# Fourier stage and first scores of the first tower's attention, put in another order

## The reference

```
y_f = fourier_mix(zf, w_fourier)      # Re(2-D DFT over positions and group channels), then @ w_f
q   = rms_norm(cq) @ w_uq             # 8 heads, 64 + 32 rope channels
k,v = rms_norm(ckv) @ w_ukv           # k gets the shared rope part kr
p   = softmax((qn.kn + rope(qr).kr) * scale);  attn = p @ v
y_c = conformer_conv(zg)              # 31-tap depthwise conv, LayerNorm, silu, pointwise
x   = x + gate * (concat([y_f, attn, y_c]) @ w_o)
```

## Time and profile before

| what | value |
|---|---|
| median of 3 runs | 2862.61 us (2860.85 to 2864.79) |
| the profiled execution | 2860.66 us, its span 2858.9 us |
| PE busy | 2749.6 us (96%) |
| DVE, ACT, POOL busy | 1693.3, 1108.4, 1123.5 us (59%, 39%, 39%) |

### The profile page before, as it was taken

One profiled execution on the slowest core, in us unless ns is written; L12 is line 12 of the kernel. 1 busy time (PEld: TensorE's weight loads), 2 busy tenths in 40 slices (PEclk: granted clock), 3 DMA queues, 4 the chain that ended last, 5 costly groups with the idle time before them and its releaser, 6 DMA issues.

```text
span 2858.9 us, 39941 instructions
## 1 busy us (share of the span) xinstructions
PE 2749.6 (96%) x14626; PEld 2217.2 (78%) x14626; DVE 1693.3 (59%) x2428; ACT 1108.4 (39%) x1815; POOL 1123.5 (39%) x533
## 2 busy tenths in 40 slices
PE   6999899999999999999999999899999999999998
PEld 3855688888888756788887688668888888888887
DVE  4978676564646577486678654856634643533133
ACT  4346533121222436542223523664433444443242
POOL 1399323333332277144444321003444434344443
PEclk8999999999999999999999999999999999999999
DMA  7600043333333320034454221003544532233332
GB/s 286 208 6 1 1 148 118 109 127 114 122 118 119 110 96 1 31 133 162 162 191 148 95 67 38 1 10 102 203 150 147 183 113 88 83 94 96 96 96 81
DMA packets 83492, 303.81 MB, mean 106 GB/s; under 512 B 9120, under 2 KB 12704, under 8 KB 82464
## 3 DMA queue, kind: packets, MB, share of 16 engines
q1 hardware_dynamic: 83072, 298.43, 30.8%
q10 hardware_dynamic: 288, 3.55, 0.3%
HBM read 299.84 MB, written 2.10 MB: 106 GB/s over the span
## 4 chain that ended last, share of the span: by engine, by line
PE 55%; DVE 6%; ACT 2%; issue 2%; POOL 0%; DVEq 0%; ACTq 0%; POOLq 0%
PE psum L1954 15%; PE psum L1751 10%; PE psum L1352 9%; PE psum L1975 8%; PE psum L1391 2%; PE psum L1829 1%; PE psum L1442 1%; PE psum L1610 1%; DVE psum L2112 1%; DVE in_lo L2105 1%; PE psum L1850 1%; DVE tiny L2620 1%; PE psum L1671 1%; DVE hidden_lo L2482 1%; PE psum L1657 1%
## 5 line engine op out<-in xcount | busy, mean ns | idle before, releaser
L642 POOL TENSOR_TENSOR w_lo<-w_raw,w_hi 128x1024 fp32r<-128x1024 f32 x346 | 868.3, 2510 | 1700.4 <-ACT w_hi L708 1700.2
L708 ACT ACTIVATE w_hi<-w_raw 128x1024 fp32r<-128x1024 f32 x346 | 366.9, 1060 | 1226.3 <-PE psum L1751 542.3
L2217 DVE CUSTOM_DVE_ANT_0 mod_w<-mod_w,conditions 128x1024 f32<-128x1024 f32 x176 | 287.4, 1642 | 4.4
L2198 DVE SCALAR_TENSOR_TENSOR residual<-psum,modulation,residual 128x512 f32<-128x512 f32 (+1 forms) x152 | 101.1, 684 | 316.6 <-PE psum L1975 143.3
L1954 PE MATMUL psum<-in_hi,w_hi 128*128 128x512 f32 x672 | 262.6, 391 | 4.4 <-DVE small_w L2704 2.5
L1954 PE MATMUL psum<-in_lo,w_hi 128*128 128x512 f32 x672 | 262.3, 390 | 0.0
L1954 PE MATMUL psum<-in_hi,w_lo 128*128 128x512 f32 x672 | 262.1, 390 | 0.0
L1751 PE MATMUL psum<-hidden_hi,w_hi 128*128 128x256 f32 (+1 forms) x736 | 223.1, 356 | 2.6 <-DVE hidden_lo L2482 2.2
L1751 PE MATMUL psum<-hidden_lo,w_hi 128*128 128x256 f32 (+1 forms) x736 | 222.2, 355 | 0.0
L1751 PE MATMUL psum<-hidden_hi,w_lo 128*128 128x256 f32 (+1 forms) x736 | 222.2, 355 | 0.0
L1751 PE MATMUL psum<-in_hi,w_hi 128*128 128x256 f32 (+1 forms) x720 | 215.5, 354 | 2.2 <-POOL w_lo L642 2.2
(11 more groups left out here) (330 smaller groups left out, 5778.1 us busy)
## 6 DMA issues: line engine op xcount, KB each, us to landing
w_raw<-stream_dram SPq DMA_DIRECT2D x346, 512.0 KB, 4.2
mod_w<-mods_dram SPq DMA_DIRECT2D x176, 512.0 KB, 3.7
mixer_space<-first_mods_dram SPq DMA_DIRECT2D x12, 512.0 KB, 14.5
small_w<-small_w_dram SPq DMA_DIRECT2D x2, 2048.0 KB, 13.1
in_hi_space<-dft_x_dram SPq DMA_DIRECT2D x2, 2048.0 KB, 8.8
residual<-tokens_dram ACTq DMA_DIRECT2D x1, 3072.0 KB, 10.6
in_lo_space<-first_mods_dram SPq DMA_DIRECT2D x4, 512.0 KB, 16.0
conditions<-conditions_dram SPq DMA_DIRECT2D x2, 1024.0 KB, 11.4
```

The costliest lines, as they stand in the source:

```text
L642: nc.gpsimd.tensor_tensor(wlo[:, (j % 2) * 1024:(j % 2 + 1) * 1024], raw3[:, j, :], whi[:, (j % 2) * 1024:(j % 2 + 1) * 1024].bitcast(F32) ...
L708: nc.scalar.activation(whi[:, (j % 2) * 1024:(j % 2 + 1) * 1024], raw3[:, j, :], ACT.Copy).then_inc(hi_ready, 1)
L2198: last = nc.vector.scalar_tensor_tensor(res3[:, m, s0:s1], bank(2 * (t % 2) + b, c1=s1 - s0), M(block_, chunk, m, 1 - b), res3[:, m, s0:s1 ...
L2217: nc.vector.tensor_tensor_reduce(w_tile, w_tile, cvec[:, 0:D], 1.0, 0.0, ALU.mult, ALU.add, dots[:, q:q + 1]).then_inc(mod_done, 1)
```

## The change

Four things move, on three engines; nothing is added to the work or taken from it, and the queues of POOL and SP are the same.

PE: the projections of the Fourier stage stand behind each position part `y`, no longer ahead of it. `scores(1)` moves from behind the products with `w_f` to ahead of them, `scores(2)` from the loop (d = 1) to behind the products, ahead of `turn(0)`. ACT: `proj_ev` moves with its projections, `exps(1)` moves from the loop (d = 0) to between the copies of the two products. DVE: `minimum(1)` moves from the loop to a place of its own in `TAPS_BEFORE` (`second`): in layer 0 three taps behind `weigh(0)`, with three more taps behind it; in layer 1 behind `rope1`. All of this holds for both layers, as the code is shared.

```diff
--- before.py
+++ after.py
@@ -444,8 +444,8 @@
             return sum(w(x) for _, x in group[:i])
 
         LN_FROM = (19, 12)
-        TAPS_BEFORE = [dict(queries=0, rope0=11, rope1=12, minimum=14, weigh=15, fourier=21),
-                       dict(queries=15, rope0=30, minimum=TAPS, weigh=TAPS, rope1=TAPS, fourier=TAPS)]
+        TAPS_BEFORE = [dict(queries=0, rope0=11, rope1=12, minimum=14, weigh=15, second=18, fourier=21),
+                       dict(queries=15, rope0=30, minimum=TAPS, weigh=TAPS, rope1=TAPS, second=TAPS, fourier=TAPS)]
 
         def fourier_out(m, seg):
 
@@ -979,20 +979,23 @@
                 segs = both(cols)
                 pieces = early_pieces(layer, 2 * len(segs))
                 for c in range(2):
-                    for _ in segs:
-                        for n in pieces.pop(0):
-                            proj_ev(n)
+                    for n in pieces.pop(0) if len(segs) > 1 else ():
+                        proj_ev(n)
                     if c:
                         exps(0)
                     act.wait_ge(s["y_mm"], c + 1)
                     for seg, _ in segs:
                         last = nc.scalar.activation(yf[:, c, seg[0]:seg[1]], fourier_out(c, seg), ACT.Copy)
                     last.then_inc(s["y_cp"], 1)
+                    for n in pieces.pop(0):
+                        proj_ev(n)
                 for m in range(2):
                     act.wait_ge(s["f_mm"], m + 1)
                     for seg, _ in segs:
                         last = nc.scalar.activation(hi3[:, m, seg[0]:seg[1]], fourier_out(m, seg), ACT.Copy)
                     last.then_inc(s["f_hi"], 1)
+                    if m == 0:
+                        exps(1)
                 for d in range(n_units + 1):
                     if d:
                         ev(d - 1)
@@ -1002,7 +1005,7 @@
                         proj_ev(before[d])
                     if d == n_units:
                         conv_silu()
-                    if d + 1 < n_units:
+                    if d and d + 1 < n_units:
                         exps(d + 1)
                     if d:
                         pv_hi(d - 1)
@@ -1618,8 +1621,6 @@
                 pieces = early_pieces(layer, 2 * len(segs))
                 for c in range(2):
                     for seg, _ in segs:
-                        for n in pieces.pop(0):
-                            project(n)
                         if c == 0:
                             pe.wait_ge(late["dft"], 32 * (layer + 1))
                         first, table = (0, dft_c) if seg == CTX else (2, dft_x)
@@ -1631,9 +1632,11 @@
                                                   256 * c + 128 * part + 128],
                                                table[:, part, k, :], start=(k == 0 and part == 0),
                                                stop=(k == nk - 1 and part == 1))
-                    mm.then_inc(s["y_mm"], 1)
-                    if c == 0:
-                        scores(0)
+                        if seg == segs[-1][0]:
+                            mm.then_inc(s["y_mm"], 1)
+                        for n in pieces.pop(0):
+                            project(n)
+                    scores(c)
                 for m in range(2):
                     for c in range(2):
                         if m == 0:
@@ -1642,7 +1645,7 @@
                             mm = pe.matmul(fourier_out(m, seg), wf[:, m, c, :],
                                            yf[:, c, seg[0]:seg[1]], start=(c == 0), stop=(c == 1))
                     mm.then_inc(s["f_mm"], 1)
-                scores(1)
+                scores(2)
                 pe.wait_ge(s["f_lo"], 2)
 
                 def turn(u):
@@ -1694,7 +1697,7 @@
                         mm.then_inc(s["ln"], 1)
 
                 for d in range(n_units + 1):
-                    if d and d + 1 < n_units:
+                    if d > 1 and d + 1 < n_units:
                         scores(d + 1)
                     if d in before:
                         project(before[d])
@@ -2411,7 +2414,7 @@
                         last.then_inc(s["ln"], 1)
 
                 steps = dict(rope0=lambda: rope_q(0), rope1=lambda: rope_q(1),
-                             minimum=lambda: minimum(0), weigh=lambda: weigh(0))
+                             minimum=lambda: minimum(0), weigh=lambda: weigh(0), second=lambda: minimum(1))
                 for step, until in TAPS_BEFORE[layer].items():
                     if step in steps:
                         taps(until)
```

## The result

The changed kernel takes 2875.35 us (median of 5 runs, 2873.43 to 2887.93) against 2861.49 us of 5 runs of the kernel before beside it: ratio 1.0052 (95%: 1.0037 to 1.0067), slower by 0.4 to 0.7%.

What follows compares the result with a forecast made beforehand. PE, busy 96% of the span, was taken as the bound, so only its waits and low clock count. Layer 1's +11.3 and layer 0's -1.7 us gave +9.6, forecast 2872.3 us, range 2866 to 2879.

Steps and rivals of the forecast that it cites:

- layer 1's bare chain: Layer 1: uncovered rotation before unit 0's scores +5.0, exponentials before unit 2's +2.6, copy before the loop's keys projection +1.4 us.
- its -1.7: Layer 0's net term: 3.0 us gained at the first value product, only 1.7 kept; bounds -7.0 and +1.3.
- the step: Layer 1, unit 0's scores: copy and rotation of head 0's queries no longer covered by the position part, +5.0 us.
- The copy of piece 3: Layer 1, ahead of head 0's query projection: PE waits for ACT to copy out the keys projection's bank, 0.6 us.
- The first clock fall: Layer 1, behind the 4.8 us idle time at unit 0's scores: the clock falls, +2.95 us, bounds 0 and 3.2.
- rival 1: More clock falls, at layer 1's unit 2 scores or layer 0's waits: +3.0 us (2875.3) or +6 (2878.3), called 2877; chance 0.27.
- the forecast's case: Whole kernel: layer 1 +11.3 us with one clock fall, layer 0 -1.7, in all 2872.3 us; chance 0.50.
- the cap: Layer 0's first LayerNorm sum: it waits for POOL's last tap, which doesn't move, so PE can gain only 1.7 us.
- Waits predicted 1.3, 1.7 and 0.8 us: Layer 0: PE waits ahead of unit 2's scores, at the turn for `lo3`, and at the first value product for ACT's copy.
- The upper bound of layer 0: Layer 0: waits around the short turn lower the clock, 3.7 us of work runs at half speed; +1.3 us.
- Rival 3: Not slower: layer 0 gets all 7.0 us back, layer 1 loses 6.2, giving 2861.8 us; not-slower chance 0.13.
- Rivals 2 and 4: Cheaper rotation, no fall in layer 1: 2868 us, 0.10; waits just move with the scores: 2862.6 us, within not-slower's 0.13.

Runs made afterwards that it cites:

- Keeping the cover: Kernel before with layer 1 in the new order, but both head 0 query projections again ahead of the first position part: 2870.31 us, ratio 1.0029.
- stilling POOL: Layer 0 old, layer 1 new, ten of POOL's layer 1 taps left out so POOL stands still beside both rotations: 2870.94 us, ratio 1.0027.

## Why the prediction came out as it did

Forecast 2872.3 us and slower; measured 2875.35. The direction and its mechanism (layer 1's bare chain) were right. The size was 3 us low, or 4.2 us as a difference: +9.6 forecast, +13.9 against the 2861.49 us of before beside it. Two terms were too low, the clock in layer 1 (+1.9) and layer 0 (its -1.7 did not come).

- **Layer 1's chain held term by term.** Predicted waits 4.8, 2.6 and 1.4 us; measured 4.86, 2.52 and 1.28. Without the clock my terms sum to 8.4 us; the stage without falls is 126.3 us against 117.90, 8.4 us. Keeping the cover took away what the step said; stilling POOL took 2.8 us, for which I had 2.2.
- **The copy of piece 3** cost 0.47 us, for which I had put 0.6.
- **The first clock fall** came, at 3.1 us in this profile for my 2.95, and at 1.7 with layer 1 alone new. The 2.95 itself read the earlier trace rows a little short: 0.83 in 190 to 195 us is low until 191.7, which gives 3.1.
- **The undersized step is the second fall in layer 1.** I left it to rival 1 ("close under the 2.65 that brought it down in layer 0"). It came in the changed kernel's profiles, another 1.7 us, and in six of the eight profiles of new orders of layer 1; with 2.40 us of wait it did not, nor with 1.18. Layer 1 so cost 13.2 and not 11.3 us. Strictly it is rival 1 (chance 0.27) that came, not the forecast's case, and that its 2875.3 us for one more fall is the measured time to a tenth is luck: the fall cost 1.7 us, not 3.0, and the rest is for the most part layer 0's missing gain.
- **Layer 0: the cap was right, its consequence missed.** Waits predicted 1.3, 1.7 and 0.8 us, measured 0.41, 1.52 and 0.69; DVE idle 7, measured 6.81. The start did better than I said: the first value product comes 38.2 us behind the last channel product, 42.2 before, 4.0 us gained for my 3.0. I wrote that POOL's last tap caps the gain at 1.7 us. In the profile it caps it at nothing: from the last channel product, the LayerNorm sum comes after 162.64 us, 162.69 before. Two things were wrong in that step. One is "POOL doesn't move": its last tap ends 162.5 us behind that product in this profile, 161.6 in the second and 161.2 with only layer 0 new, against 160.8 in before; but the old order gave 157.8 to 162.6, so the runs show that POOL's end varies, and not that the change moves it. The other is that a capped gain is idle time: PE arrives 3.2 us early, stands still, and the clock falls twice, once for 1.8 us in the sum and, after it was back at 1.00, behind the 2.40 us wait for ACT, 1.3 us in the value product and 0.3 in the turn. These, with 0.25 us of longer waits, are, to a tenth, the 3.5 us by which this profile's layer 0 is longer than before's. That layer 0 costs time in general isn't shown (new order 194.1 to 196.0 us, old order 191.5 to 195.7; medians 2863.1 against 2861.84). What is shown is that the 1.7 us did not come.
- **The upper bound of layer 0** (+1.3) rested on a fall behind the two waits at the start. In the changed kernel's two profiles there was none; with only layer 0 new there was, behind 0.92 and 0.69 us. The bound's sum was also uneven: 3.0 us gained less 3.7 lost is +0.7, where I wrote 1 and then 1.3.
- **Rival 3** asked for POOL to end before 305 us or not to be waited for. With three taps left out POOL ended at 291.84 us, and layer 0 took 1.3 us less than before's, not 7.0; with the sum a unit later 1.5 less. The kernel would have been slower even then.
- **Rivals 2 and 4** did not come: in the changed kernel the rotation kept its slow price, and layer 1's waits moved as the order said.

What stays open: why a wait of 2.2 to 2.7 us brings the clock down in one execution and not in another, why POOL's last tap and layer 0 as a whole scatter by 4 us in the same order, and what makes the untouched stretch between the layers 10 us longer in some executions.

## What to carry to other kernels

Before a wait is moved, follow the whole chain behind the moved producer: here the position part looked like plain work ahead of the projections, but it covered a copy and a rotation, and no engine's busy share shows that. A gain on PE ahead of a bound set elsewhere is not kept and not merely lost: it becomes idle time, and the clock can charge for it, as it did in every profile here with that wait. Where executions scatter more than the effect, compare the length of a stage on PE's timeline between two fixed instructions, take several profiles of the unchanged order to see how far that stage scatters by itself (layer 1 by 0.01 us here, layer 0 by 4), and keep what only it shows apart from what the medians show.

## What the runs showed of the hardware

- In these two stages of the fourteen profiles each of the nine waits of 3.2 us and more, and each of the eleven of 2.84 to 2.86 us, was followed by a low granted clock. Of the eight of 2.65 or 2.66 us seven were, all four of 2.51 or 2.52 us, two of three of 2.40 to 2.42 us, the one of 2.35, one of three of 2.32 us, four of six of 2.22 or 2.23 us, and one each of 1.87 and 1.78 us; none from 1.64 down to 1.04 us was, but once two waits of 0.92 and 0.69 us with 0.66 us of work between them were. A fall cost 1.6 to 3.4 us, by how soon the clock came back.
- DVE's two-input operation on 32x512 took 0.68 to 0.69 us with POOL still and up to 1.65 us beside its addition, which itself took 1.77 us there and 1.26 alone; the first operation of each rotation in layer 1 kept 0.68 us beside it.
- The same 128x512 matmuls, at a granted clock of 1.00 and without waits, took a mean of 391 ns in some executions and 395 to 403 ns in others.
